# Order of small steps in a two-block transformer kernel: shift and scale of the first layer, values of the windowed attention

## The reference, cut to what matters

```
c_act = jax.nn.silu(c)
shift, scale, gate = jnp.split(c_act @ mod_w[i] + mod_b[i], 3, axis=-1)
h = _rms_norm(x, norm_g[i]) * (1.0 + scale[:, None, :]) + shift[:, None, :]
y = _retention(h, positions, ret_w_in[j], ret_w_out[j])      # begins with h @ w_in
```

```
for window, dilation in DILATED_PAIRS:
    o, l = dilated_window_attention(qh, kh, vh, window, dilation)
weights = jax.nn.softmax(jnp.stack(lses, axis=0), axis=0)
y = jnp.sum(weights[..., None] * jnp.stack(outs, axis=0), axis=0)
```

## Time and profile before

| | us |
|---|---|
| median of 3 runs | 701.35 |
| lowest, highest | 699.55, 702.24 |
| the profiled execution | 699.93 |
| its span, first to last instruction | 698.1 |
| granted clock of TensorE, mean | 0.998 |
| PE busy in the span | 683.9 (98%) |
| DVE busy | 493.3 (71%) |
| ACT busy | 380.5 (55%) |

### The profile page before, as it was taken

The page is one execution under the profiler, slowest core; times in us unless marked ns, Lnnn a source line. Parts: engine busy times, 40 slices in busy tenths (PEclk is TensorE's granted clock), DMA queues, the critical chain, the costliest instruction groups (busy, mean ns, idle before and its releaser), DMA issues.

```text
span 698.1 us, 11642 instructions
## 1 busy us (share of the span) xinstructions
PE 683.9 (98%) x4673; PEld 556.1 (80%) x4673; DVE 493.3 (71%) x723; ACT 380.5 (55%) x561; POOL 16.2 (2%) x34
## 2 busy tenths in 40 slices
PE   7799999999999999999999999999999999999996
PEld 3679997777878888877778877778888888888885
DVE  4788998787986779765668889766666555555445
ACT  5447533565655565644665765845574454444344
POOL 6000000000000000000000000000000000000000
PEclk9999999999999999999999999999999999999999
DMA  9999875566996277832455654433656655555511
GB/s 296 367 380 354 292 259 174 202 222 230 301 336 211 61 239 230 279 125 92 128 151 154 187 174 130 143 121 95 213 177 195 195 182 182 186 186 194 188 60 61
DMA packets 74405, 138.81 MB, mean 199 GB/s; under 512 B 5732, under 2 KB 18400, under 8 KB 74352
## 3 DMA queue, kind: packets, MB, share of 16 engines
q1 hardware_dynamic: 72816, 134.92, 58.7%
q10 hardware_dynamic: 736, 1.81, 0.7%
q0 software_dynamic: 800, 1.35, 0.6%
HBM read 137.01 MB, written 1.05 MB: 198 GB/s over the span
## 4 chain that ended last, share of the span: by engine, by line
PE 93%; ACT 2%; DVE 2%; DMA 1%; SPq 1%; issue 1%; DVEq 0%; ACTq 0%
PE G L392 24%; PE G L394 23%; PE G L393 23%; PE T L433 5%; PE G L412 2%; PE G L414 2%; PE G L413 2%; DMA raw<-in_ret_w_in_dram 1%; PE T L806 1%; PE T L794 1%; PE G L529 1%; PE G L531 1%; PE G L530 1%; DVE wlo L1133 1%; PE T L924 1%
## 5 line engine op out<-in xcount | busy, mean ns | idle before, releaser
L1133 DVE TENSOR_TENSOR wlo<-raw,whi 128x1024 fp32r<-128x1024 f32 x202 | 245.7, 1221 | 116.8 <-ACT whi L1932 116.1
L1932 ACT ACTIVATE whi<-raw 128x1024 fp32r<-128x1024 f32 x202 | 212.1, 1060 | 133.3 <-PE G L394 90.1
L392 PE MATMUL G<-whi,ahi 128*128 128x512 f32 x694 | 280.5, 404 | 0.0
L394 PE MATMUL G<-whi,alo 128*128 128x512 f32 x694 | 271.0, 391 | 0.0
L393 PE MATMUL G<-wlo,ahi 128*128 128x512 f32 x694 | 270.4, 390 | 0.0
L392 PEld LDWEIGHTS G<-whi,ahi 128*128 128x128 f32 x694 | 130.3, 188 | 28.6 <-DVE wlo L1133 1.6
L394 PEld LDWEIGHTS G<-whi,alo 128*128 128x128 f32 x694 | 130.2, 188 | 28.5
L393 PEld LDWEIGHTS G<-wlo,ahi 128*128 128x128 f32 x694 | 130.5, 188 | 25.4 <-issue 1.0
L1934 ACT ACTIVATE arena<-T,st 128x128 f32<-128x128 f32 (+2 forms) x56 | 21.7, 477 | 32.3 <-DVE st L1528 32.3
L1932 ACT ACTIVATE ahi<-T 128x512 fp32r<-128x512 f32 x25 | 15.0, 598 | 40.6 <-PE T L433 40.6
L1934 ACT ACT_TABLE_LOAD x27 | 34.6, 1283 | 3.3 <-issue 1.8
(11 more groups left out here) (258 smaller groups left out, 621.2 us busy)
## 6 DMA issues: line engine op xcount, KB each, us to landing
raw<-in_ret_w_in_dram SPq DMA_DIRECT2D x48, 512.0 KB, 5.5
raw<-in_w_gate_up_dram SPq DMA_DIRECT2D x40, 512.0 KB, 3.7
raw<-in_mod_w_dram SPq DMA_DIRECT2D x32, 512.0 KB, 4.8
raw<-in_fox_w_in_dram SPq DMA_DIRECT2D x32, 512.0 KB, 4.7
raw<-in_w_in_dram SPq DMA_DIRECT2D x28, 512.0 KB, 3.6
raw<-in_w_down_dram SPq DMA_DIRECT2D x22, 512.0 KB, 3.5
arena<-in_mod_w_dram SPq DMA_DIRECT2D x16, 512.0 KB, 9.9
raw<-in_ret_w_out_dram SPq DMA_DIRECT2D x16, 512.0 KB, 6.0
```

The costliest lines, as they stand in the source:

```text
L392: e.matmul(o, ah, wh, start=first and k == 0, stop=False)
L394: done = e.matmul(o, al, wh, start=False, stop=last and k == 1)
L1133: e.tensor_tensor(o, a, b, op).then_inc(sig[name], 1)
L1932: d = e.activation(o, a, f, scale=scale)
```

## The change

Four edits. (1) The values of the windowed attention come two groups at a time, at steps 3, 5 and 7, and the second of each two uses PSUM bank T0 instead of T3. The forgetting attention keeps its order. (2) On PE the sums of group 2 move between the two products of tile 2. (3) On DVE, in group 2, the weights' low part and the first x tile's low part come ahead of the second x tile's shift and scale; in groups 3 and 4 the weights' low part comes ahead of both shifts and scales. (4) POOL waits for the first four `mod0` counts, which is after `modulated(1)`, before it issues its later loads.

```diff
-def attention_steps(n):
-    return [[("flip", i - 1)] * (1 <= i <= n) + [("logits", i + z) for z in range(2)] * (i < n and i % 2 == 0) + [("values", i - 2)] * (i >= 2)
-            for i in range(n + 2)]
+def attention_steps(n, paired):
+    return [[("flip", i - 1)] * (1 <= i <= n) + [("logits", i + z) for z in range(2)] * (i < n and i % 2 == 0)
+            + ([("values", i - 3 + z) for z in range(2)] * (i >= 3 and i % 2 == 1) if paired else [("values", i - 2)] * (i >= 2)) for i in range(n + 2)]
...
                 products(u + 2, 0, (4, 5, None), k, k == 0, k == 6)
-                if k in (2, 4):
+                if k < 6:
                     shift_scale(2 + k // 2)
                 products(u + 2, 1, (4, 5, None), k, k == 0, k == 6)
-                if k == 0:
-                    shift_scale(2)
...
-                t = bank((name, "values", g), sig[f"{name}_out"], 2 * g + 2, 3)
+                t = bank((name, "values", g), sig[f"{name}_out"], 2 * g + 2, 0 if name == "win" and g % 2 else 3)
...
                 ring_to(u - 1)
                 mod_sums(g, 0, 4)
                 mod_sums(g, 4, VECTOR_ROWS[g])
-                modulated(k)
-                modulated(k + 1)
+                if g == 2:
+                    modulated(k)
                 ring_to(u)
+                if g > 2:
+                    modulated(k)
+                    modulated(k + 1)
                 x0_low(k)
+                if g == 2:
+                    modulated(k + 1)
                 x0_low(k + 1)
                 ring_to(u + 1)
...
             fill(acc[:, :], 0.0, "acc_zero")
+            on_.wait_ge(sig["mod0"], 4)
             e.dma_start(posi, pos_in.partition_broadcast(P).rearrange("p a n -> p (a n)")).then_inc(sig["small_in"], 16)
```

More of the change, by code:

```diff
@@ L829, in win_values @@
                 values("win", WIN, g, PTw, vaw)
-            steps = attention_steps(len(FOX))
+            steps = attention_steps(len(FOX), False)
             fox = {"logits": fox_logits, "flip": lambda g: flip("fox", g, PBf), "values": fox_values}
@@ L1001, in _ @@
                 freed(0, m, "vaw", m + 1)
-            steps = attention_steps(len(WIN))
+            steps = attention_steps(len(WIN), True)
             win = {"logits": win_logits, "flip": lambda g: flip("win", g, PBw), "values": win_values}
```

## The result

The kernel after takes **704.45 us** (median of 4 runs, 703.76 to 705.09). The kernel before, run beside it, takes 700.81 us (4 runs, 699.55 to 702.24). The ratio is 1.0051, with a 95% interval of 1.0033 to 1.0068: slower by 3.6 us. The forecast was 701.2, with a range up to 703.6, so it is wrong. The profiled execution of after took 703.76 us, with a span of 702.0, against 699.93 and 698.1 before.

The account below looks back on a forecast made before the run. PE bounds the kernel from 100 us on; at the start it waits for DVE and ACT chains. Start +0.94, GpSimd's loads -0.1, values by twos -1.06 sum to -0.2: 701.35 becomes 701.2 us, range 699.2 to 703.6.

Parts of the forecast that it names:

- Group 2, PE's added wait: PE's order at tile 2: group 2's sums wait with 6 matmuls queued behind; up to 1.5 us free.
- wrong altogether: Closing sign: the forecast fails if PE's granted clock fell or a wait on T0 appeared in step 4 or 7.
- Groups 2 to 4, DVE and ACT: Start: tile 3 1.15 us earlier, gain lost; tile 6 0.48 late, tile 9 0.94 late to the end, bounds 0.5 to 1.5.
- The slower rival: DVE and ACT chain runs on past tile 10, so PE waits there too: +1.1 us, 702.5; chance 0.25.
- the rival's place: `wlo` of tiles 10 and 11; decides if `wlo` of tile 10 is more than 1.5 us late.
- Values by twos: Windowed attention: six value blocks become three, 2.38 us saved less 1.32 added, 1.06 us gain; 0.1 with pauses inside pairs.
- GpSimd's loads: POOL's loads moved behind tile 1: 0.1 us gain taken, bounds 0 to 0.8.
- The rival of the rows of group 2 landing late: Group 2: rows landing after 26.7 delay PE's sums, first `AB` and tile 3's `wlo`; up to 0.5, 701.7; chance 0.05.

Follow-up runs that it names:

- a_no_pool_wait: The changed kernel without GpSimd's (POOL's) wait for the `mod0` counts: 704.35 us (12 runs), ratio 1.0034.
- a_filler: The changed kernel plus 8 useless 512-column matmuls between the first half of tile 2's products and group 2's sums: 700.66 us, ratio 1.0005.
- pairs_pool: The kernel before with values by twos and GpSimd's wait, without the new orders of the start: 699.23 us, ratio 0.9979.
- b_start_order: The kernel before with the new orders of the start on both PE and DVE, nothing else: 705.86 us, ratio 1.007.
- b_pe_only: The kernel before with PE's new order alone, group 2's sums between tile 2's two products: 705.13 us, ratio 1.0058.
- b_fewer: The kernel before with 10 of the 16 warming matmuls ahead of the first sums left out: 706.46 us, ratio 1.0075.
- b_early_wait: The kernel before, old order, with one added PE wait for group 2's rows between the halves of tile 2's products: 706.57 us, ratio 1.0075.
- a_padded: The changed kernel with 12 more, shorter warming matmuls, same columns in all (24 more PE instructions): 704.99 us, ratio 1.0051.
- b_pool_wait: The kernel before with GpSimd's wait alone, ahead of its load of the positions: 700.59 us, ratio 0.9993.
- b_padded: The kernel before with 12 more, shorter warming matmuls, same columns in all: 701.29 us, ratio 1.0001.

## Why the prediction was wrong

- **Group 2, PE's added wait: this step failed.** The prediction said that "a wait of up to 1.5 us there is free", since nobody wants the 6 matmuls behind it before 29.5. It looked only at what work was queued behind the wait. It put the wait's effect on the load of PE's next instructions at nothing, without a word on it, and that load came 4.3 us late (29.21 for 24.91). PE itself lost 0.31 us by the wait (its row at 25.29); by the late load it lost 4.7, and 0.95 by the clock, which fell at the end of the stop (31.2). I had written that I would be wrong altogether if PE's granted clock fell, but as a thing apart, with no case for what could make it fall.
- **Groups 2 to 4, DVE and ACT: right.** Without the stop (a_no_pool_wait), tiles 3, 4, 6 and 9 start within 0.2 to 0.3 us of the forecast (29.28, 32.83, 41.40, 52.60), with the forecast's waits: PE behind `wlo` at tile 4 (0.57, forecast 0.8), behind the sums and `alo` at tiles 6 and 9. The forecast had tiles 6 and 9 0.48 and 0.94 late, and they are 0.27 and 0.71 late there; VectorE's order alone makes them 0.8 and 1.25 late.
- **The slower rival** (the chain runs on past tile 10) is not what made after slow. In the change without the stop tile 12 starts at 60.85, 0.72 behind before's 60.13, and tile 9 was 0.71 behind: nothing grows past it. Where VectorE's lateness was larger something does grow, but later than the rival's place: from 1.3 to 2.1 us with VectorE's order alone and from 1.1 to 1.6 in a_filler, both between 77 and 83 us. For the result the rival had the right sign by another mechanism.
- **Values by twos: right in form, too large in size.** The sum took 0.83 for a block behind logits, of which 0.33 was an idle time before the block. That idle stays when the block goes. Two blocks stood behind logits: 1.06 - 2 x 0.33 = 0.40 for them all; measured 0.63. For the 0.23 between them I have no row. The prediction had asked whether the idle belongs to a block's first wait or to the change of form; the third answer, that it belongs to the end of the logits, was not among its cases, though going from logits to a product is a change of form too. Its row where products follow logits directly (447.92 and 449.01, no idle) spoke against that, but it stands behind 16 loads and not 8.
- **GpSimd's loads: perhaps too small.** Tiles 1 and 3 come 1.5 and 1.2 us earlier in the profile of the wait alone, and 0.24 and 0.26 in that of pairs_pool, for 0.1 taken and 0.8 as the bound; in the time it is -0.5 (0.9982 to 1.0005), not to be told from nothing.
- **The rival of the rows of group 2 landing late** (chance 0.05) looked at the right place: they land at 25.2, and PE does wait for them. Its price was worked out from the sums alone.

The range was worked out from the cases, and none of them had a stop of PE; its width for the spread of runs ended at 703.6.

## What to carry to other kernels

A wait that costs the engine nothing by the work behind it can still hold up the engine's own instructions: before you put one ahead of a stretch of many short instructions, look in the trace for the loads on the instruction queue, and see that the queue is not standing at an open wait when one is due. An idle of "issue" of several us inside a run of like instructions, with an instruction packet that lands shortly before its end, is that case; useful work (or even useless work) in front of the wait, or fewer short instructions behind it, cured it here. Ask of every pause in the rows what it follows as well as what it precedes, before you count it as saved.

## What the runs showed of the hardware

- PE's instructions come by DMA in packets of 16 KB, in 1.1 us each at this place; with SP's queue full, a second load that was held up by a wait begins 3.9 to 4.1 us after that wait is met, and PE resumes 1.3 to 1.4 us after it has landed.
- PE ran dry each time after 695 or 696 matmuls and weight loads, in streams with 24 more or 20 fewer instructions ahead of the sums too; 32-column matmuls (29 started in 0.25 us) use up fast what is there.
- In every profile with a stop of 3.6 to 5.2 us the granted clock falls to the 1.2 GHz level, during the stop or within 0.5 us behind it: for 3.41 us in after, for 6.83 in b_start_order, b_pe_only, b_fewer and b_early_wait, and for 10.24 (from 27.65) in a_padded. The profiles of b_pool_wait and b_padded have one such stretch of 3.41 us without a stop (mean clock 0.995 and 0.996), and that of before has none (0.998). By their mean clock, about half of before's runs have one: 701.1 to 702.2 us with it, 699.5 to 700.4 without (one at 700.08 has 0.995); that is most of its spread.
